# Chunked scan of a Mamba-2 layer: rows of running sums spread by DMA from device memory instead of by 64 TensorE products

## The reference, cut to what matters

```
da = dt * a;  cs = cumsum(da) within a chunk
decay[l, s] = exp(cs[l] - cs[s])  for s <= l, else 0
y_diag = ((C_l . B_s) * decay[l, s]) @ (x * dt)
states = B^T @ (x * dt * exp(cs[end] - cs))
y_off  = (C @ previous state) * exp(cs)
y      = y_diag + y_off + D * x,  then y * silu(z), RMSNorm, output projection
```

## Time and profile before

| | |
|---|---|
| median of 3 runs | 1679.56 us (1677.16 to 1680.3) |
| the profiled execution | 1678.3 us |
| its span in the profile | 1676.2 us |
| mean granted TensorE clock | 0.977 of full speed |
| PE, DVE, ACT, POOL busy | 92%, 26%, 13%, 6% of the span |
| chain that ended last | PE 80%, DMA 8%, DVE 6%, issue 4%, ACT 1% |
| DMA | 485.74 MB, mean 290 GB/s |
| ACT's DMA queue (q10) | 1.33 MB, all of it at the start |

### The profile page before, as it was taken

The page is one execution under the profiler, slowest core; times in us unless marked ns, Lnnn a source line. Parts: engine busy times, 40 slices in busy tenths (PEclk is TensorE's granted clock), DMA queues, the critical chain, the costliest instruction groups (busy, mean ns, idle before and its releaser), DMA issues.

```text
span 1676.2 us, 23905 instructions
## 1 busy us (share of the span) xinstructions
PE 1544.0 (92%) x10681; PEld 906.2 (54%) x10682; DVE 429.9 (26%) x895; ACT 215.0 (13%) x411; POOL 106.1 (6%) x129
## 2 busy tenths in 40 slices
PE   7887999999999999989999998999999889977975
PEld 5644487777588766546343353356666643423322
DVE  6796212232255455222000001010010010100202
ACT  3311300000321143220000000000000000000001
POOL 7164000000000011000000000000000000000000
PEclk9997999999999999998999999999999999999999
DMA  9576386664564403255999986999999969999996
GB/s 339 177 247 236 139 302 244 234 224 169 181 228 151 151 1 143 109 206 216 404 408 409 391 296 259 403 408 408 402 406 395 377 250 404 407 409 403 408 407 240
DMA packets 167297, 485.74 MB, mean 290 GB/s; under 512 B 12928, under 2 KB 15872, under 8 KB 167168
## 3 DMA queue, kind: packets, MB, share of 16 engines
q1 hardware_dynamic: 162624, 482.51, 75.4%
q10 hardware_dynamic: 4544, 1.33, 0.4%
HBM read 482.78 MB, written 1.05 MB: 289 GB/s over the span
## 4 chain that ended last, share of the span: by engine, by line
PE 80%; DMA 8%; DVE 6%; issue 4%; ACT 1%; POOL 0%; DVEq 0%; SPq 0%; POOLq 0%; ACTq 0%
PE bank L1753 26%; PE bank L1280 21%; PE bank L1784 13%; DMA ring<-in_moe_w_down 5%; PE bank L1483 5%; PE bank L1673 3%; DMA ring<-in_moe_w_gate 3%; PE bank L1593 3%; PE bank L1725 2%; PE bank L1287 1%; DVE arena L982 1%; PE bank L1765 1%; PE bank L1632 1%; DVE arena L990 1%; PE bank L1608 1%
## 5 line engine op out<-in xcount | busy, mean ns | idle before, releaser
L1753 PE MATMUL bank<-ring,arena 128*32 128x256 f32 (+3 forms) x3664 | 387.0, 432 | 42.1 <-issue 27.0
L1753 PEld LDWEIGHTS bank<-ring,arena 128*32 128x32 f32 (+1 forms) x3664 | 179.4, 121 | 238.6 <-issue 182.0
L1280 PE MATMUL bank<-arena,ring 128*128 128x256 f32 x1264 | 282.8, 384 | 1.4 <-ACT arena L674 1.0
L1280 PEld LDWEIGHTS bank<-arena,ring 128*128 128x128 f32 x1264 | 240.9, 193 | 34.4 <-ACT arena L674 1.7
L1784 PE MATMUL bank<-ring,arena 128*32 128x256 f32 (+1 forms) x1792 | 208.1, 459 | 16.1 <-DMA ring<-in_moe_w_down 15.3
L1202 DVE TENSOR_TENSOR arena<-arena,bank 128x512 f32<-128x512 f32 (+2 forms) x44 | 24.4, 577 | 658.6 <-PE bank L1753 658.6
L1784 PEld LDWEIGHTS bank<-ring,arena 128*32 128x32 f32 (+1 forms) x1792 | 87.4, 121 | 127.4 <-issue 90.8
L1753 PE MATMUL bank<-arena 128*32 128x256 f32 (+3 forms) x1200 | 116.1, 402 | 9.8 <-issue 4.0
L788 ACT ACTIVATE arena<-bank 128x512 f32<-128x512 f32 (+2 forms) x44 | 21.1, 508 | 645.5 <-PE bank L1765 549.1
L1753 PEld LDWEIGHTS bank<-arena 128*32 128x32 f32 (+1 forms) x1200 | 57.9, 121 | 65.8 <-issue 49.9
L1483 PE MATMUL bank<-ring,arena 128*128 128x512 f32 x176 | 76.9, 595 | 1.5 <-PE bank L1280 1.5
(11 more groups left out here) (274 smaller groups left out, 1240.5 us busy)
## 6 DMA issues: line engine op xcount, KB each, us to landing
ring<-in_moe_w_down SPq DMA_DIRECT2D x46, 2048.0 KB, 19.3
ring<-in_moe_w_up SPq DMA_DIRECT2D x45, 2048.0 KB, 23.6
ring<-in_moe_w_gate SPq DMA_DIRECT2D x41, 2048.0 KB, 23.7
ring<-in_ada_w SPq DMA_DIRECT2D x24, 2048.0 KB, 9.5
arena<-in_moe_w_gate SPq DMA_DIRECT2D x15, 2048.0 KB, 23.6
ring<-in_m_w_in SPq DMA_DIRECT2D x12, 2048.0 KB, 9.0
arena<-in_moe_w_up SPq DMA_DIRECT2D x11, 2048.0 KB, 23.6
arena<-in_moe_w_down SPq DMA_DIRECT2D x10, 2048.0 KB, 21.7
```

The costliest lines, as they stand in the source:

```text
L1280: ins = mm(out_, l, r, start=i == 0, stop=i == len(pairs) - 1, **kw)
L1753: ins = mm(ps[base + b // per][m * h:m * h + m, w * (b % per):w * (b % per) + w], hcur3[:, kc, m * b:m * b + m], sl[:, kc - half * rows, w ...
```

## The change

The running sums are computed once more, at n == 4 of the projection loop, with `da` as the stationary and `tri` as the moving operand: two products (four records) that give 64 rows (32 heads x 2 blocks) of 128 sums, in bank 6. ACT copies them to SBUF (`csrow`) and stores them, 32 KB, into a tensor in device memory laid out as 16 rows of 512, one for each step of the scan. During the projection loop (n = 27 to 29) and then in steps 1 to 13 ACT issues sixteen loads, each of which reads one row of 2 KB to all 128 partitions of a `dmin` buffer (256 KB in SBUF). `dmin` has three buffers in place of two. DVE's four subtractions read and write `dmin` in place, in SBUF, after a wait for the load. The 64 spreading products, and PE's waits for `dec_min`, are gone. The load of step n + 2 is issued by ACT after its Exp of step n, behind a wait for `m_ready` of `mixed(n - 1)`, whose buffer it overwrites.

```diff
-        dmin = area(13312, 2, HALF)
+        dmin = area(13312, HALF), area(13312 + HALF, HALF), area(18688, HALF)
+        csrow = area(19200, P)[0:NB * HEADS]
+        cs_rows = nc.dram_tensor("cs_rows", (NB * NG, HALF), F32, kind="Internal").ap()
...
+            def load_decay(n):
+
+                if n == 0:
+                    act.wait_ge(s["cs_saved"], 16)
+                if n >= 3:
+                    act.wait_ge(s["m_ready"], n - 2)
+                act.dma_start(dmin[n % 3], cs_rows[n:n + 1, :].broadcast_to([P, HALF])).then_inc(s[f"dec_in{n % 3}"], 16)
             for n in range(32):
...
                 if n == 4:
                     act.wait_ge(s["cs_mm"], 1)
+                    act.wait_ge(s["ada_turned"], turn_of(2 * NADA - 1) + 1)
+                    c.then(f(csrow, ps[6][0:NB * HEADS, 2 * P:3 * P], ACT.Copy), "cs_row")
+                    act.dma_start(cs_rows.rearrange("n (j l) -> (n j) l", j=4), csrow).then_inc(s["cs_saved"], 16)
                     c.inc(f(hd[:, ECS:TOEND + 1], ps[6][:, P:2 * P].rearrange("p (k b h) -> p k b h", k=2, b=NB), ACT.Exp), "cs_exp")
...
+                if 27 <= n <= 29:
+                    load_decay(n - 27)
             for n in range(NB * NG):
                 act.wait_ge(s["dec_min"], n + 1)
-                c.inc(f(dmin[:, n % 2], dmin[:, n % 2], ACT.Exp), "dec_exp")
+                c.inc(f(dmin[n % 3], dmin[n % 3], ACT.Exp), "dec_exp")
+                if 1 <= n < NB * NG - 2:
+                    load_decay(n + 2)
...
-                dve.wait_ge(s["dec_mm"], n + 1)
+                dve.wait_ge(s[f"dec_in{n % 3}"], 16 * (n // 3 + 1))
                 blk, grp = n // NG, n % NG
                 for j in range(4):
                     at = 4 * grp + j
-                    ins = ts(dmin[:, n % 2, P * j:P * j + P], ps[n % 2][:, P * j:P * j + P],
+                    ins = ts(dmin[n % 3][:, P * j:P * j + P], dmin[n % 3][:, P * j:P * j + P],
                              hd[:, NCS, blk, at:at + 1], 0.0, ALU.add, ALU.min)
...
                     pe.wait_ge(s["da_ready"], 1)
+                    for b in range(NB):
+                        mm(ps[6][HEADS * b:HEADS * b + HEADS, 2 * P:3 * P], hd[:, DA, b], tri[:, :], start=True, stop=True)
...
             for n in range(NB * NG):
                 blk, grp = n // NG, n % NG
-                if n >= 2:
-                    pe.wait_ge(s["dec_min"], n - 1)
-
-                da = hd[:, DA, blk, 4 * grp:4 * grp + 4]
-                dec = bank(n % 2, 4, P)
-                for j in range(4):
-                    ins = mm(dec[:, j], da[:, j:j + 1].broadcast_to([P, P]), tri[:, :], start=True, stop=True)
-                ins.then_inc(s["dec_mm"], 1)
                 if n:
                     pe.wait_ge(s["cbm_ready"], n)
...
             y_products(NB * NG - 1)
-            pe.wait_ge(s["dec_min"], NB * NG)
-
             pe.wait_ge(s["cbm_ready"], NB * NG)
```

More of the change, by code:

```diff
@@ L283, in hybrid_trunk @@
             xbc_mm conv_done silu_done xs_turned xs_ready b_turned1 btok_ready z_mm z_silu
-            dec_mm dec_min dec_exp cb_mm cbm_ready m_ready xw_ready xdt_ready y1_mm st_mm st_ready y_ready
+            cs_row cs_saved dec_in0 dec_in1 dec_in2 dec_min dec_exp cb_mm cbm_ready m_ready xw_ready xdt_ready y1_mm st_mm st_ready y_ready
             y_turned yT1_a yT1_b logit_mm rt_pre rt_exp
@@ L1069, in mixed @@
                     dve.wait_ge(s["y1_mm"], n - 1)
-                c.inc(tt(mix[:, n % 2].rearrange("p (j l) -> p j l", j=4), dmin[:, n % 2].rearrange("p (j l) -> p j l", j=4),
+                c.inc(tt(mix[:, n % 2].rearrange("p (j l) -> p j l", j=4), dmin[n % 3].rearrange("p (j l) -> p j l", j=4),
                          cbm[:, n % 2:n % 2 + 1].broadcast_to([P, 4, P]), ALU.mult), "m_ready")
```

## The result

| | before | changed |
|---|---|---|
| median (runs) | 1679.56 us (5) | 1665.69 us (5) |
| lowest to highest | 1677.16 to 1681.11 | 1664.19 to 1670.08 |
| profiled execution, its span | 1678.3, 1676.2 | 1665.08, 1663.0 |
| mean granted clock | 0.977 | 0.981 |

The median is 13.9 us lower, at 1665.69 where 1665.6 was forecast. The ratio is 0.9925, 95% interval 0.9914 to 0.9936, which is 12.6 us less (10.7 to 14.4).

The account below looks back on a forecast made before the run. PE was taken to bound the scan loop; 14.24 - 0.49 - 0.44 = 13.3 us saved gives 1665.0 from the profiled execution or 1666.3 from the median, forecast 1665.6 between them. Range 1662 to 1671.5 us.

Parts of the forecast that it names:

- Part one: Scan loop of layer 1: sixteen groups of four spreading products leave PE's chain, 0.89 us each, 14.2 us saved.
- Part two: Head of the loop: PE newly idles for DVE's mask product before the second C·B, 0.49 us lost.
- Part three: Projection loop at n == 4: two added products, four records, on PE, 0.44 us lost.
- Part four: ACT at n == 4: added copy, wait and DMA issue, about 0.8 us, hidden in ACT's idle stretches.
- Part five: The sixteen 256 KB loads: 0.49 us of ACT per issue, landing in 2 to 3 us, costing nothing.
- the line through two other rows: Latency estimate for a 256 KB load, from a 512 KB store and a 2 MB load: 1.8 us.
- The room of 8.1 us: Block 0 of the scan: time from a load's possible issue to DVE's subtraction using it; 8.7 in block 1.
- Rival 1: Loads in block 1 queue behind weight transfers, 9.7 us each, 3.5 us in all: 1669 us, chance 0.07.
- Rival 2: ACT bounds the scan loop through issues of 4.09 us each: 1683 us, slower than before, chance 0.04.
- Rival 3: The expert weights' stream alone sets the end, which doesn't move with the loop: 1678 us, chance 0.03.
- The range's high end: Whole kernel: the median's 1666.3 with loads queued at the low price and two more for clock or late load: 1671.5.

Follow-up runs that it names:

- a3: The changed kernel with the 64 spreading products issued as well, into banks nobody reads: 1679.62 us, ratio 1.0003 to the kernel before.
- a1: The changed kernel run again, nothing edited: 1665.42 us, ratio 0.9922 to the kernel before.
- c1: The changed kernel with the C·B product in the two freed PSUM banks, PE waiting for the mask product of step n - 2: 1664.05 us, one execution.
- b1: The changed kernel with two dmin buffers in place of three: 1673.16 us, ratio 0.9962 to the kernel before.
- a4: The kernel before with each spreading product issued twice, 128 in place of 64: 1693.87 us, ratio 1.0091 to the kernel before.
- b2: The changed kernel with two more unused 256 KB loads issued by ACT in each of steps 1 to 13: 1673.44 us, ratio 0.9958 to the kernel before.

## Why the prediction was right

**Part one held.** The 14.2 us of spreading products were on the path and came back one to one. Measured between a3 and a1 the loop's difference is 12.69; with the 0.71 that the products cover at the head it is 13.40 for 15 groups, 0.89 each.

**Part two was too small.** It had 0.49 us for the head of the loop, and the idle time itself was 0.45 to 0.5. From the start of the first C·B product to the z product after the second it is 588.90 - 587.74 = 1.16 with the wait and 0.45 without (c1): 0.71. What I left out is that the product after the wait costs about 0.25 us beside the idle time; the same stood in the earlier trace rows, where the y group after 0.30 us of idle time has 1.07 in place of 0.84.

**Part three was a little small:** 0.54 us in place of 0.44. In the kernel before the sums' products and their neighbours take 0.81 in the chain at n == 4, in the changed one 1.35. The four added records are 0.34 of the difference; the neighbours account for the rest.

**Part four held.** The copy took 0.25 us, the store's issue 0.51, and Silu of n = 5 still waited for DVE, 0.59 us in both kernels.

**Part five held, with wrong sizes that didn't matter.** A load alone took 3.0 to 3.2 us (3.5 once), where I took 2 to 3 and the line through two other rows gave 1.8; the bounds were 1.8 and 22.5. Its issue cost ACT 0.33 us, not 0.49. The room of 8.1 us was worked out rightly, as b1 shows from the other side: less a step of it, block 1 fails and block 0 just holds. The 2.6 us that the Trainium skill's fit gives ("DMA: Bandwidth & Descriptors", "Anatomy of one DMA"), as an estimate, were under the 3.0 as well; the page gives that fit for DMAs issued by gpsimd, which I had not said, and these loads are ACT's.

**Rival 1 named a real effect, and its price was half right.** In the changed kernel a load issued 2.1 to 3.7 us after a weight transfer takes 4.7 to 6.3 us in place of 3.1. I had added the whole transfer and the whole load, 9.7 us. But SP's transfer starts when PE frees a z tile, and ACT's load 3.7 us later (632.31 and 636.02, 642.82 and 646.52), so the first part of the transfer is over by then: 4.7 and 5.7 us are left of the sum, inside the room of 8.7. And of the seven loads I counted as exposed only these two met a transfer in that way; the others found none, or one that was 8.7 us old. On the Trainium skill's rule in "Issuing engines are not separate DMA queues": that ACT's load has no engines of its own, the trace bears out, since the load of 646.52 moved nothing while the transfer held the time of all 16. What I drew from "interleave", that it would get its turns inside the transfer, holds for b1's load issued 0.8 us after one, and not for this load, which moved when all but 0.11 MB of the transfer was through. Why the one got its turns and the other did not stays open. The sum stayed as it was for another reason than the one I gave. **Rival 2** fell by 0.33 us an issue. **Rival 3** fell by a3 and a4.

**Sum.** With the measured terms the change is worth 14.24 - 0.71 - 0.54 = 13.0 us, and 13.9, 13.5 and, by a3 against a1, 14.2 were measured by the medians; the ratios give 12.6 (10.7 to 14.4) and 13.1 (9.6 to 16.8). The forecast of 13.3 and the corrected 13.0 can't be told apart by that. That the profiled execution came out within 0.1 us of the forecast is partly luck: stages that the change doesn't touch moved by about 2 us each and cancelled. The range's high end, added up as it was described, is 1666.3 + 3.5 + 2 = 1671.8 and not 1671.5, which decides nothing here.

## What to carry to other kernels

A product that only copies a row to all partitions costs the engine that bounds the stage. Here a DMA from device memory did it for nothing, because its latency, measured beside the traffic of that stage, fitted into the time from the free buffer to the use. Work out that room before the edit, count a load that is issued in the first microseconds of a large transfer as landing with it, and choose the number of buffers by that: one fewer lost half of the gain here. And look at stages, not at totals, when an experiment changes the data that a later stage branches on.

## What the runs showed of the hardware that I had not expected

- A 256 KB load of one 2 KB row to 128 partitions took 3.0 to 3.2 us in the changed kernel (3.5 once). Its latency beside a 2 MB transfer of the other queue went by how old the transfer was. Issued 0.8 to 4.6 us after it, the load landed between 0.9 us before and 1.1 us after it (nineteen loads). Issued 6.0 us or more after it, the load took 3.0 to 3.4 us (ten loads). In b2, with three loads a step, transfers grew to 10.5 to 13.1 us and loads landed up to 3.1 us ahead of them.
- A product that follows a wait costs about 0.25 us more than its idle time: groups of 0.49 for 0.22, and 1.07 for 0.84.
- The same kernel had granted clocks of 1.00 and 0.68 at the same product in two executions, 1.6 us apart from A to B, and they ended 0.9 us apart.
- Four float32 subtractions of 128 columns took 0.86 us with SBUF as their source and 1.12 with PSUM.
